# Depthwise convolution of a long fp32 block: order of loads, taps, moves and sums around it, and the layer norm's root

## What is computed

```python
def conformer_conv(x, w_pw1, b_pw1, w_dw, b_dw, ln_g, ln_b, w_pw2, b_pw2):
    h = x @ w_pw1 + b_pw1
    a, gate = jnp.split(h, 2, axis=-1)
    h = a * jax.nn.sigmoid(gate)
    h = lax.conv_general_dilated(h, w_dw[:, None, :], window_strides=(1,), padding=[(CONV_WIDTH - 1, 0)],
        dimension_numbers=('NWC', 'WIO', 'NWC'), feature_group_count=D_MODEL) + b_dw   # 31 taps a feature
    h = jax.nn.silu(layer_norm(h, ln_g, ln_b))
    return h @ w_pw2 + b_pw2
```

## Time and profile before

| | us |
|---|---|
| median of 3 runs (2649.66 to 2652.07) | 2651.91 |
| the profiled execution | 2651.03 |
| its span from first to last instruction | 2649.2 |
| PE busy in it | 2539.1 (96%) |
| PEld (weight loads) busy | 2006.5 (76%) |
| DVE busy | 1055.7 (40%) |
| ACT busy | 710.8 (27%) |
| POOL busy | 997.0 (38%) |
| granted TensorE clock, mean | 0.98 of full |

### The profile page before, as it was taken

The page is one execution under the profiler, slowest core; times in us unless marked ns, Lnnn a source line. Parts: engine busy times, 40 slices in busy tenths (PEclk is TensorE's granted clock), DMA queues, the critical chain, the costliest instruction groups (busy, mean ns, idle before and its releaser), DMA issues.

```text
span 2649.2 us, 30280 instructions
## 1 busy us (share of the span) xinstructions
PE 2539.1 (96%) x11680; PEld 2006.5 (76%) x11680; DVE 1055.7 (40%) x1579; ACT 710.8 (27%) x912; POOL 997.0 (38%) x322
## 2 busy tenths in 40 slices
PE   7998999989999999889999999999999889999998
PEld 5766787667888888448888888888888666888886
DVE  5473715548422316765223111422311465522301
ACT  2333223323222222132222222222222354222221
POOL 3421343213444342004444444444444554444442
PEclk9999999999999999989999999999999889999999
DMA  3221132212222222412222233322224001222232
GB/s 141 107 79 64 64 112 88 80 40 80 95 95 90 88 98 101 118 50 96 95 95 80 98 107 127 128 95 95 86 87 170 22 1 48 96 95 95 80 98 75
DMA packets 42034, 235.83 MB, mean 89 GB/s; under 512 B 5345, under 2 KB 5345, under 8 KB 21473
## 3 DMA queue, kind: packets, MB, share of 16 engines
q1 hardware_dynamic: 41808, 232.60, 25.4%
q10 hardware_dynamic: 144, 2.10, 0.2%
HBM read 222.86 MB, written 6.29 MB: 86 GB/s over the span
## 4 chain that ended last, share of the span: by engine, by line
PE 87%; DVE 6%; issue 3%; ACT 2%; POOL 0%; SPq 0%; DMA 0%; DVEq 0%; ACTq 0%; POOLq 0%
PE ps L1338 26%; PE ps L1340 26%; PE ps L1339 26%; PE ps L1687 2%; PE ps L1612 1%; PE ps L1698 1%; PE ps L1545 1%; PE ps L1581 1%; PE ps L1574 1%; PE ps L1673 1%; DVE conv_out L1225 1%; PE ps L1524 1%; DVE tmp L1225 1%; PE ps L1533 1%; PE ps L1352 1%
## 5 line engine op out<-in xcount | busy, mean ns | idle before, releaser
L481 POOL TENSOR_TENSOR w_lo<-raw,w_hi 128x2048 fp32r<-128x2048 f32 (+1 forms) x212 | 901.9, 4254 | 1548.8 <-ACT w_hi L579 1548.8
L1338 PE MATMUL ps<-x_hi,w_hi 128*128 128x512 f32 x2048 | 809.3, 395 | 20.2 <-DVE x_lo L848 17.7
L1340 PE MATMUL ps<-x_hi,w_lo 128*128 128x512 f32 x2048 | 799.6, 390 | 0.0
L1339 PE MATMUL ps<-x_lo,w_hi 128*128 128x512 f32 x2048 | 799.0, 390 | 0.0
L579 ACT ACTIVATE w_hi<-raw 128x2048 fp32r<-128x2048 f32 (+1 forms) x220 | 385.5, 1752 | 359.2 <-PE ps L1340 344.3
L1338 PEld LDWEIGHTS ps<-x_hi,w_hi 128*128 128x128 f32 x2048 | 385.8, 188 | 111.8 <-issue 28.6
L1340 PEld LDWEIGHTS ps<-x_hi,w_lo 128*128 128x128 f32 x2048 | 385.5, 188 | 81.8
L1339 PEld LDWEIGHTS ps<-x_lo,w_hi 128*128 128x128 f32 x2048 | 386.3, 189 | 77.1
L958 DVE TENSOR_TENSOR tmp<-ps,rms_b 128x512 f32<-128x512 f32 x88 | 60.9, 692 | 589.2 <-PE ps L1340 578.7
L1338 PE MATMUL ps<-hid_hi,w_hi 128*128 128x512 f32 x704 | 278.1, 395 | 0.0
L1340 PE MATMUL ps<-hid_hi,w_lo 128*128 128x512 f32 x704 | 278.1, 395 | 0.0
(11 more groups left out here) (192 smaller groups left out, 2480.7 us busy)
## 6 DMA issues: line engine op xcount, KB each, us to landing
raw<-in_w_up SPq DMA_DIRECT2D x88, 1024.0 KB, 4.9
raw<-in_w_down SPq DMA_DIRECT2D x64, 704.0 KB, 4.1
raw<-in_w_feat SPq DMA_DIRECT2D x24, 1024.0 KB, 4.9
raw<-in_w_pw SPq DMA_DIRECT2D x12, 1024.0 KB, 5.0
raw<-in_w_tok SPq DMA_DIRECT2D x8, 1024.0 KB, 5.0
raw<-in_w_out SPq DMA_DIRECT2D x8, 1024.0 KB, 4.9
shifted<-conv_in SPq DMA_DIRECT2D x80, 67.5 KB, 2.0
bias<-in_bias_t SPq DMA_DIRECT2D x8, 512.0 KB, 6.1
```

Source lines behind the costliest of these rows:

```text
L481: nc.gpsimd.tensor_tensor(w_lo[:, s, 0:w], raw[:, s, 0:w], w_hi[:, s, 0:w].bitcast(f32), ALU.subtract).then_inc(lo_ready, 1)
L1338: nc.tensor.matmul(out, hi, src_hi, start=start, stop=False, skip_group_check=True)
L1339: nc.tensor.matmul(out, hi, src_lo, start=False, stop=False, skip_group_check=True)
L1340: return nc.tensor.matmul(out, lo, src_hi, start=False, stop=stop, skip_group_check=True)
```

## The change

1. SP: the loads of pw2's chunks 0 and 1 stand ahead of the copies of m = 2 instead of behind them.
2. DVE, gate loop: `gate(c)`, then three taps (not for c = 0), `gated(c)`, then `low` of chunk c+2, then taps until ten a round are done. In the last round three taps stand behind `gated`, too.
3. ACT: the move of PE's tile m = 0 stands in the gate loop, ahead of the sigmoid of chunk 7.
4. POOL adds six of the eight convolved tiles (PE's m = 0 to 3, DVE's 0 and 1) into `conv_total`, which shares its memory with `tmp[:, 5]`, with five adds of 128x512. PE's mean is now three matmuls behind all taps: the total, DVE's tile 2, PE's m = 4.
5. Root of the variance on one partition (1x512), turned to `[128, 4]` by four matmuls, reciprocal on `[128, 4]`, back to a row in every partition by `rows_of` into bank 5; the multiplies read that bank.

```diff
-TAPS_A_CHUNK = 9
+TAPS_A_CHUNK = 10
+TAPS_UNDER_GATE = 3
...
+    ln_inv_t = small[:, 10:14]
...
+    conv_total = tmp[:, 5, :]
...
         for m, j in enumerate(CONV_ON_PE):
+            if m == 2:
+                stream("pw2", w_pw2, 0, 1)
             sp.wait_ge(conv_gated, m + 1)
...
-            if m == 2:
-                stream("pw2", w_pw2, 0, 1)
...
+                pool.wait_ge(conv_moved, 1)
+                pool.wait_ge(conv_summed, 1)
+                nc.gpsimd.tensor_tensor(conv_total, conv_out[:, CONV_ON_PE[0], :], conv_out[:, CONV_ON_DVE[0], :],
+                                        ALU.add).then_inc(conv_total_made, 1)
+                added = 1
+                for on_pe, j in ((True, 1), (False, 1), (True, 2), (True, 3)):
+                    pool.wait_ge(conv_moved if on_pe else conv_summed, j + 1)
+                    pool.wait_ge(conv_total_made, added)
+                    part = conv_out[:, (CONV_ON_PE if on_pe else CONV_ON_DVE)[j], :]
+                    nc.gpsimd.tensor_tensor(conv_total, conv_total, part, ALU.add).then_inc(conv_total_made, 1)
+                    added += 1
...
-        layer("pw1", gate_in_place("pw1", ACT.Sigmoid, "b_pw1"), norm=True)
+        def conv_move(m):
+            act.wait_ge(conv_done, m + 1)
+            nc.scalar.activation(conv_out[:, CONV_ON_PE[m], :], ps[:, 4 + m % 2, :], ACT.Identity,
+                                 bias=col("b_dw", CONV_ON_PE[m])).then_inc(conv_moved, 1)
+
+        def pw1_finish(i, s, gate=gate_in_place("pw1", ACT.Sigmoid, "b_pw1")):
+            if isinstance(i, int) and i == KD // 2 - 1 and s:
+                conv_move(0)
+            gate(i, s)
+
+        layer("pw1", pw1_finish, norm=True)
         high_part("pw2", 0, 1)
-        for m, j in enumerate(CONV_ON_PE):
-            act.wait_ge(conv_done, m + 1)
-            nc.scalar.activation(conv_out[:, j, :], ps[:, 4 + m % 2, :], ACT.Identity, bias=col("b_dw", j))\
-                .then_inc(conv_moved, 1)
+        for m in range(1, len(CONV_ON_PE)):
+            conv_move(m)
...
-        nc.scalar.activation(rms_b[:, :], ps[:, 6, :], ACT.Sqrt, scale=1.0 / D_MODEL, bias=eps_ln)\
+        nc.scalar.activation(rms_b[0:1, :], ps[0:1, 6, :], ACT.Sqrt, scale=1.0 / D_MODEL, bias=eps_ln[0:1])\
             .then_inc(ln_root, 1)
...
         for c in range(KD):
             gate(c)
+            if c:
+                taken = taps_until(taken + TAPS_UNDER_GATE)
+            gated(c)
+            if c + 1 == KD:
+                taken = taps_until(taken + TAPS_UNDER_GATE)
             if c + 2 < KD:
                 low(name, c + 2)
             else:
                 low("pw2", c + 2 - KD)
-            gated(c)
-            until = TAPS_A_CHUNK * (c + 1) if c + 1 < KD else n_taps
-            for n in range(taken, until):
-                tap_of(CONV_ON_DVE[n // CONV_WIDTH], n % CONV_WIDTH)
-            taken = until
+            taken = taps_until(TAPS_A_CHUNK * (c + 1) if c + 1 < KD else n_taps)
...
-        dve.wait_ge(ln_root, 1)
-        then(nc.vector.reciprocal(rms_b[:, :], rms_b[:, :]))
+        dve.wait_ge(ln_turned, 1)
+        nc.vector.reciprocal(ln_inv_t, ps[:, 4, 0:ST]).then_inc(ln_inv, 1)
         dve.wait_ge(centred, KD)
+        dve.wait_ge(ln_rows, 1)
         for j in range(KD):
-            nc.vector.tensor_tensor(conv_out[:, j, :], conv_out[:, j, :], rms_b[:, :], ALU.mult)\
+            nc.vector.tensor_tensor(conv_out[:, j, :], conv_out[:, j, :], ps[:, 5, :], ALU.mult)\
                 .then_inc(ln_scaled, 1)
...
         for m in range(1, len(CONV_ON_PE)):
             tile_taps(m)
-            add_to_mean(CONV_ON_PE[m - 1], start=m == 1)
-            if m >= 2:
-                add_to_mean(CONV_ON_DVE[m - 2])
-        add_to_mean(CONV_ON_PE[-1], stop=True).then_inc(mean_rows, 1)
+        pe.wait_ge(conv_total_made, len(CONV_ON_PE) + len(CONV_ON_DVE) - 3)
+        nc.tensor.matmul(ps[:, 7, :], ones[:, :], conv_total, start=True, stop=False)
+        pe.wait_ge(conv_summed, len(CONV_ON_DVE))
+        nc.tensor.matmul(ps[:, 7, :], ones[:, :], conv_out[:, CONV_ON_DVE[-1], :], start=False, stop=False)
+        pe.wait_ge(conv_moved, len(CONV_ON_PE))
+        nc.tensor.matmul(ps[:, 7, :], ones[:, :], conv_out[:, CONV_ON_PE[-1], :], start=False, stop=True)\
+            .then_inc(mean_rows, 1)
...
+        pe.wait_ge(ln_root, 1)
+        for c in range(ST):
+            ins = nc.tensor.matmul(ps[:, 4, c:c + 1], rms_b[0:1, P * c:P * (c + 1)], ones[0:1, 0:1],
+                                   start=True, stop=True)
+        ins.then_inc(ln_turned, 1)
+        pe.wait_ge(ln_inv, 1)
+        rows_of(ln_inv_t, 5, ln_rows)
```

More of the change, by code:

```diff
@@ L320, in build @@
     ln_root = semaphore("ln_root")
+    ln_turned = semaphore("ln_turned")
+    ln_inv = semaphore("ln_inv")
+    ln_rows = semaphore("ln_rows")
+    conv_total_made = semaphore("conv_total_made")
     ln_hi = semaphore("ln_hi")
@@ L1234, in _, with taps_until @@
         taken = 0
+        def taps_until(until):
+            for n in range(taken, until):
+                tap_of(CONV_ON_DVE[n // CONV_WIDTH], n % CONV_WIDTH)
+            return until
         for c in range(KD):
             gate(c)
+            if c:
[3 more added lines that the diff above has]
+                taken = taps_until(taken + TAPS_UNDER_GATE)
             if c + 2 < KD:
@@ L1622, in _ @@
         layer("pw1", "pw1", "pw1", after_pair=taps_after)
-        def add_to_mean(j, start=False, stop=False):
-            if j in CONV_ON_PE:
-                pe.wait_ge(conv_moved, CONV_ON_PE.index(j) + 1)
-            else:
-                pe.wait_ge(conv_summed, CONV_ON_DVE.index(j) + 1)
-            return nc.tensor.matmul(ps[:, 7, :], ones[:, :], conv_out[:, j, :], start=start, stop=stop)
         for m in range(1, len(CONV_ON_PE)):
             tile_taps(m)
-            add_to_mean(CONV_ON_PE[m - 1], start=m == 1)
-            if m >= 2:
-                add_to_mean(CONV_ON_DVE[m - 2])
-        add_to_mean(CONV_ON_PE[-1], stop=True).then_inc(mean_rows, 1)
+        pe.wait_ge(conv_total_made, len(CONV_ON_PE) + len(CONV_ON_DVE) - 3)
[5 more added lines that the diff above has]
+            .then_inc(mean_rows, 1)
         for j in range(KD):
```

## The result

| | before | changed |
|---|---|---|
| median, us (lowest to highest, executions) | 2650.78 (2646.18 to 2652.07, 4) | 2628.36 (2626.51 to 2637.89, 4) |
| profiled execution, us; its span | 2651.03; 2649.2 | 2627.77; 2626.0 |
| ratio, 95% interval | | 0.9923 [0.9905, 0.9941] |

The account below looks back on a forecast made before the run. PE, carrying 87% of the span, was taken as the bound. An earlier last tap (16.6 us) plus the root (0.6) gave 17.2, so 2651.03 became 2633.8, or 2634.7 against the median; range 2631 to 2641.

Parts of the forecast that it names:

- the one from the profiled span to the median and the range: Whole kernel: 17.2 us off 2651.03 gives 2633.8, plus 0.9 gives 2634.7 against the median; range 2631 to 2641.
- last tap earlier: PE's convolution: no gaps from chunk 5 to the last tap, which comes 16.6 us earlier.
- the wait at m = 0: PE ahead of the first shifted tile's taps: earlier gated(3) lets copies land in time, removing 1.14 us idle.
- root to first multiply: Layer norm: the one-row root takes 3.1 to 4.9 us against 4.11; 3.5 taken, a gain of 0.6.
- clock back earlier behind the norm: PE at pw2's start: half clock expected to stay, nothing counted; 3.1 us more if full clock were kept.
- DVE's round: DVE's gate loop: three taps fill the 2.10 us wait; round 12.22 becomes 10.8 us, under PE's 10.99.
- Adds on GpSimd: Five adds at 1.28 us each, costing DVE at most 6.4 us; priced at zero, with 2.6 us of slack.
- rival 1: DVE ends the convolution, slowed by GpSimd's adds: gain 6 to 13, chance 0.13; under 5.3, chance 0.03.
- Rival 3: The clock falls in PE's row of narrow taps: a loss of 7 us, 2659; chance 0.02.
- Rival 2: Reorder pays less in the gate loop, late remainders or m=4 copies: gain 11 to 14, about 2639; chance 0.12.
- Rival 4: Clock kept into pw2, or both small chains at full clock: gain 18 to 21, about 2632; chance 0.15.
- The move in the loop: ScalarE empties bank 4 before tile 2 needs it, helping remove PE's 7.95 us gap before the mean.

Follow-up runs that it names:

- e10: Changed kernel with ScalarE's move of PE's first tile put back behind the gate loop; convolution 193.36 us, median 2632.13 us, ratio 0.9930.
- e12: e11 plus 16 matmuls without use in the thin start of the attention stage; attention 244.40 us, median 2627.11 us, ratio 0.9913.
- e1: The kernel before, run and profiled again with no edit; convolution 209.72 us, attention 233.95 us, median 2648.78 us, ratio 1.0003.
- second pair: Both kernels profiled again with no edit; convolution 209.72 us before and 192.10 us changed, a difference of 17.62 us.
- e11: Changed kernel with 21 filler matmuls ahead of pw2 and m = 0's copies ahead of pw1's last load; convolution 189.97 us, median 2627.53 us.
- e5: Changed kernel with pw2's two loads put back behind the copies of m = 2; convolution 195.39 us, median 2629.16 us, ratio 0.9926.
- e8: Changed kernel without GpSimd's five adds, the mean back on PE between the tap tiles; convolution 198.17 us, median 2631.84 us, ratio 0.9952.
- e7: Changed kernel with DVE's old gate loop, no taps under the gate; convolution 201.17 us, median 2639.96 us, ratio 0.9969.
- e9: Changed kernel with each of GpSimd's five adds done twice; convolution 196.73 us, median 2638.22 us, ratio 0.9958.
- e6: Kernel before with only pw2's two loads moved ahead of the copies of m = 2; convolution 200.09 us, median 2642.84 us, ratio 0.9962.
- e4: Changed kernel with the full-width root and reciprocal of before; convolution 193.39 us, median 2628.01 us, ratio 0.9919.
- e3: Changed kernel with 20 matmuls without use between the turned root and pw2; convolution 190.80 us, median 2624.73 us, ratio 0.9907.

## Why the prediction was wrong in its number and right in its mechanism

**The failed step is the one from the profiled span to the median and the range**: "From 2651.03 that is 2633.8; the median shown lies 0.9 above the profiled run, so against it 2634.7". It took every part outside the convolution as fixed, and the range of 2631 to 2641 held only what the convolution could do. The profiled execution of the changed kernel, 2627.77, lies 6.0 us under that 2633.8: 8.48 by a shorter attention stage, 0.65 by the convolution and 0.4 by the rest, less 3.56 by a longer start. Where nothing is edited, up1 to q repeats within 0.06 us over all fourteen profiles, while attention reads 233.8 to 234.0 in eight of them and 242.3 to 242.5 in four (e10 and e12 lie elsewhere), and the start 1010.65 to 1015.16. The 64 executions of before in these comparisons, e1's ten not counted, show it: 24 lie at 2641.5 to 2646.2, 39 at 2649.7 to 2655.5, and one between. The first three executions of before, all that was shown ahead of the prediction, lay in the upper group, and by their times (2626.5 to 2628.9, and 2637.9) three of the first four of the changed kernel had the short form. The profile of before can't show that an execution has another form; but attention's granted clock of 0.89, in a stage with 1105 matmuls between waits, was there to be read, and a low end 8.5 us under the forecast, at 2626, would have held the result.

**The convolution, term by term**, each from the pw1 reciprocal:

| term | forecast | measured |
|---|---|---|
| last tap earlier | 16.6 | 16.3 (130.1 to 113.8) |
| of it the wait at m = 0 | 1.14 | 0.36 (1.14 to 0.78) |
| root to first multiply | 0.6 (3.5 left) | 0.79 (3.32 left) |
| clock back earlier behind the norm | 0 | about 0.8, by chance |
| stretch | 17.2 | 17.85; second pair 17.62 |

- *The wait at m = 0* was mis-sized: "m=0's copies land before PE is through chunk 5, and the 1.14 us go". gated(3) did come early, at 1056.7 (1053.2 on the clock of before, whose pw1 reciprocal is 3.56 us earlier; forecast 1053.3), but SP stands at the load of pw1's last chunk until the remainder of chunk 5 is done at 1058.9:

```profile
1011.63 47.81 SPq L390 DMA_DIRECT2D raw<-in_w_pw  x5
1059.65 21.21 SPq L451 DMA_DIRECT2D shifted<-conv_in  x32
```

  The copies start at 1059.65. The remainder was moved behind three taps and gated, and a queue behind it was not followed. e11 puts the copies first, and the wait goes. Of the 0.8 us missed (1.14 - 0.36), 0.4 come back from four tiles that take 27.6 us in a row instead of the 4 x 7.0 reckoned.
- *DVE's round*: 10.69 us from L1212 to L1212 (1031.16, 1041.85, 1052.54), forecast 10.8 to 11. Right.
- *Adds on GpSimd*: taken as 1.28 us each, which is the length of an add that need not wait (1.27 in e5). With their waits the five read 11.1 us, 2.2 on average (1.69, 4.33 for two, 1.80, 3.26). The prediction let rival 1 decide "from 1.8 us an add", and these adds are above that; yet it did not decide, because DVE pays not an add's recorded length but 1.03 us for each (1.77 - 0.74), five times 5.2, forecast at most 6.4. A remainder beside the first add read 3.38 instead of 2.29. The last sum ends at 1125.86, that is 1122.3 on the clock of before, forecast 1122.4; PE takes it from 1128.97. So the term stayed zero, with 3.1 us of slack (forecast 2.6). That the end came to 0.1 us is luck: without adds (e8) DVE ends at 1117.2 on the clock of before and not at 1116, and the smaller toll made up for it. The Trainium skill (SBUF — State Buffer, "SBUF: two separate sides") says that whichever of the two starts first gets the shared pair for its whole instruction and the other fully blocks. The traces agree: beside an add a DVE tap gets longer by 1.03 us. That an add may be passed over by many taps one after another, as e7's was for 11.86 us, the page does not say.
- *Rival 3* (clock falls in the taps): 1.00 in all windows. *Rival 2* (gate loop pays less): only the 0.8 us of m = 0. *Rival 1*: not in the changed kernel, but e7 and e9 show how near it is. *Rival 4*: only in part. Both small chains ran at full clock, 1.05 and 1.16; the clock then fell before pw2. It is back 4.4 us behind pw2's first matmul instead of 6.1, worth the 0.8 above. No run shows that as an effect of the shorter idle time: with the full-width root and its 9.80 us wait this took 6.1, 4.8, 5.7 and 3.6 us (before, e1, e6, e4), with the turned root 4.4 and 2.7 in the same kernel and up to 5.7 in e9. e3's filler takes it away.
- *The move in the loop* was summed together with the loads, in one term of 7.95 us. e6 and e10 part them: the loads alone bring that term, and the move adds nothing beside them.

## What to carry to other kernels

Cut the span at operations that the change doesn't touch and compare stretch by stretch before a total is explained; and when a forecast is set against a median, look which stages of the profile run with a clock between its two levels, since their length is not a constant of the kernel. Where an edit moves a wait on one engine, follow every queue that waits for the work moved back, SP's loads too: here a remainder put behind three taps held the copies that the edit was to bring forward. Adds on GpSimd beside a VectorE that never pauses are not priced by their own length alone: each cost VectorE 1.03 us here, and the last one was held back until VectorE's row ended, by 2 us in the changed kernel and 10.6 in e7. Leave that much slack behind the last add; a gap in the row or an earlier last add was not tried.

## What was not expected of the hardware

- The attention stage has two lengths, 233.9 and 242.4 us, for the same instructions in the same kernel, with 37.5 and 54.6 us at half clock (e10 lies between, at 239.15 and 47.7). Half of the difference in time at half clock is the difference in length.
- An add of GpSimd, 1.8 us among taps that let it in, took 11.86 us beside 16 taps of VectorE issued back to back, though each of these lasts only 0.74 us.
- A root on one partition takes 0.68 us, the same as the one on 128 partitions, 0.69: what the turned root saves is the wide reciprocal, 3.35 us against 0.18.
